# Level products of a gated recurrence in 32 by 32 blocks, and three fill products moved

## The reference

```python
b = cumsum(log_f, axis=1)
decay = exp(where(causal, b[:, :, None] - b[:, None, :], -inf))
scores = einsum('btshd,bshd->bhts', q[:, :, None] * decay, k)
o = einsum('bhts,bshv->bthv', scores, v) + einsum('bthd,bhdv->bthv', q * exp(b), state)
new_state = exp(b_end)[..., None] * state + einsum('bshd,bshv->bhdv', k * exp(b_end[:, None] - b), v)
```

## Time and profile before

| | |
|---|---|
| runs of the kernel before | 2424.71, 2426.08, 2427.40 us (median 2426.08) |
| profiled execution | 2427.41 us; its span, first to last instruction, 2425.6 us |
| TensorE busy | 2325.3 us, 96% |
| VectorE, ScalarE, GpSimd busy | 1211.8, 703.2, 644.4 us |
| mean granted TensorE clock | 0.984 of 2.4 GHz |

### The profile page before, as it was taken

One profiled execution on the slowest core, in us unless ns is written; L12 is line 12 of the kernel. 1 busy time (PEld: TensorE's weight loads), 2 busy tenths in 40 slices (PEclk: granted clock), 3 DMA queues, 4 the chain that ended last, 5 costly groups with the idle time before them and its releaser, 6 DMA issues. The chain is left out here.

```text
span 2425.6 us, 37166 instructions
## 1 busy us (share of the span) xinstructions
PE 2325.3 (96%) x14722; PEld 2194.6 (90%) x14722; DVE 1211.8 (50%) x2110; ACT 703.2 (29%) x1428; POOL 644.4 (27%) x725
## 2 busy tenths in 40 slices
PE   6999999999999999889999898979999999999997
PEld 6989999999999999778879898979899899898896
DVE  4125699999970776255543545154233233232335
ACT  5224412221221223344544323242122122121221
POOL 3453522122312876200001212142121212121213
PEclk9999999999999999999999999989999999999999
DMA  5351223232325443522116433231111111111104
GB/s 164 108 133 58 66 81 96 82 102 82 99 85 166 143 121 86 159 83 87 57 39 202 155 113 99 75 122 54 51 38 48 42 44 44 43 51 36 52 18 156
DMA packets 208951, 214.64 MB, mean 88 GB/s; under 512 B 32624, under 2 KB 190064, under 8 KB 208816
## 3 DMA queue, kind: packets, MB, share of 16 engines
q1 hardware_dynamic: 208816, 212.80, 28.1%
HBM read 153.34 MB, written 59.43 MB: 88 GB/s over the span
## 5 line engine op out<-in xcount | busy, mean ns | idle before, releaser
L249 POOL TENSOR_TENSOR w_lo<-w_raw,w_hi 128x2048 fp32r<-128x2048 f32 (+2 forms) x41 | 174.3, 4252 | 634.5 <-ACT w_hi L242 634.5
L2452 POOL TENSOR_TENSOR w_lo<-w_raw,w_hi 128x2048 fp32r<-128x2048 f32 x31 | 142.9, 4608 | 589.5 <-ACT w_hi L2476 589.5
L262 PE MATMUL ps<-f_hi,w_hi 128*128 128x384 f32 (+1 forms) x768 | 251.4, 327 | 2.4 <-POOL ff_u_lo L2448 2.4
L262 PE MATMUL ps<-f_hi,w_lo 128*128 128x384 f32 (+1 forms) x768 | 251.4, 327 | 0.0
L262 PE MATMUL ps<-f_lo,w_hi 128*128 128x384 f32 (+1 forms) x768 | 251.2, 327 | 0.0
L262 PE MATMUL ps<-h_hi,w_lo 128*128 128x384 f32 (+1 forms) x768 | 250.6, 326 | 0.0
L262 PE MATMUL ps<-h_lo,w_hi 128*128 128x384 f32 (+1 forms) x768 | 250.5, 326 | 0.0
L262 PE MATMUL ps<-h_hi,w_hi 128*128 128x384 f32 (+1 forms) x768 | 250.4, 326 | 0.0
L623 ACT ACTIVATE b_stage<-ps 128x256 f32<-128x256 f32 (+4 forms) x203 | 84.8, 418 | 526.6 <-PE ps L262 526.6
L2529 DVE TENSOR_TENSOR big<-big,ps 128x512 f32<-128x512 f32 x144 | 99.0, 688 | 271.9 <-PE ps L262 271.9
L262 PE MATMUL ps<-w_hi,h_hi 128*128 128x256 f32 (+1 forms) x792 | 226.2, 286 | 3.5 <-PEq L488 3.5
(11 more groups left out here) (226 smaller groups left out, 5475.1 us busy)
## 6 DMA issues: line engine op xcount, KB each, us to landing
w_raw<-in_w_in SPq DMA_DIRECT2D x34, 1024.0 KB, 5.5
w_raw<-in_w_up SPq DMA_DIRECT2D x16, 1024.0 KB, 5.3
w_raw<-in_w_down SPq DMA_DIRECT2D x16, 1024.0 KB, 5.1
gm_gate<-d_gate SPq DMA_DIRECT2D x48, 192.0 KB, 2.5
d_gate<-gatef_stage SPq DMA_DIRECT2D x28, 192.0 KB, 3.4
gm_y_raw<-d_y SPq DMA_DIRECT2D x8, 576.0 KB, 5.0
n_x<-in_x_prompt SPq DMA_DIRECT2D x8, 512.0 KB, 7.6
w_raw<-in_w_mem_kv SPq DMA_DIRECT2D x4, 1024.0 KB, 5.9
```

The costliest lines, as they stand in the source:

```text
L249: engine.tensor_tensor(g.w_lo[:, s, 0:size], g.w_raw[:, s, 0:size], g.w_hi[:, s, 0:size].bitcast(F32), ALU.subtract).then_inc(g.w_split, 1)
L262: last = pe.matmul(out, left(a, kk), right(b, kk), start=(kk == 0 and n == 0), stop=(kk == k - 1 and n == 2))
L2452: G.tensor_tensor(g.w_lo[:, slot, :], g.w_raw[:, slot, :], g.w_hi[:, slot, :].bitcast(F32), ALU.subtract).then_inc(g.w_split, 1)
```

## The change

Levels 1 to 16 are made as 32 by 32 products: for each head and each block of 32 tokens, keys of the block by queries of the block, written to that block's 32 output partitions and to columns j x 32 of the bank, so that one bank holds all six heads. One predicated copy a level, with masks of 32 columns, puts them into a compact tile `sdiag` (cleared once by GpSimd), and after level 16 VectorE copies the 4 (tile 8: 2) diagonal blocks from it into `smat` and signals `d_done`, for which the read-out now waits. Levels 32 and 64 are made as blocks of first-half keys by second-half queries and kept by plain copies, one for each block. A level takes one bank, and VectorE waits for its own copy of the level before. The masks are loaded by four DMAs. In the attention the 3 fill matmuls stand behind `mem_turn` and `q_turn`.

```diff
--- before.py
+++ after.py
@@ -1065,6 +1065,10 @@
     return levels(i) + ["q", "k"]
 
 
+DIAG = 32
+NEAR = [h for h in LEVELS if 2 * h <= DIAG]
+
+
 PER_TILE = len(LEVELS) + 2
 
 
@@ -1107,7 +1111,8 @@
         ybT = sb("ybT", [P, B_HEADS, P])
         ms, expo = sb("ms", [P, B_HEADS]), sb("expo", [P, B_HEADS])
         state = [sb("stateP", [P, B_HEADS, HD]), sb("stateS", [P, B_HEADS, HD])]
-        masks = sb("masks", [P, len(LEVELS) - 1, P], I32)
+        sdiag = sb("sdiag", [P, 2, B_HEADS, DIAG])
+        masks = sb("masks", [P, len(NEAR), DIAG], I32)
 
         sem = lambda name: g.sem("hr_" + name)
         masks_in, state_in, s_cleared = sem("masks_in"), sem("state_in"), sem("s_cleared")
@@ -1116,7 +1121,7 @@
         k_ready, q_ready = [sem("k_ready0"), sem("k_ready1")], [sem("q_ready0"), sem("q_ready1")]
         t_ready = [sem("t_ready0"), sem("t_ready1")]
         lv_done, lv_free, qk_done, qk_free = sem("lv_done"), sem("lv_free"), sem("qk_done"), sem("qk_free")
-        sq_done, rs_done, o_normed = sem("sq"), sem("rs"), sem("o_normed")
+        sq_done, rs_done, o_normed, d_done = sem("sq"), sem("rs"), sem("o_normed"), sem("d_done")
 
         LV_BANK, N_LV, QK_BANK, N_QK = 4, 4, 2, 2
 
@@ -1129,7 +1134,7 @@
             if tick in STEP_AT:
                 i, pos = STEP_AT[tick]
                 if pos < len(levels(i)):
-                    lv += 1 if pos == len(levels(i)) - 1 else 2
+                    lv += 1
                     lv_of[i, pos] = lv
                 else:
                     qk += 2
@@ -1185,7 +1190,9 @@
                 sp.dma_start(heads(wide(bg, i)), features(g.d_bg, i)).then_inc(v_in[i % 3], 16)
 
             load_first(0)
-            sp.dma_start(masks[:], io["c_masks"][:, 0:len(LEVELS) - 1, :]).then_inc(masks_in, 16)
+            for k0 in range(0, P, DIAG):
+                sp.dma_start(masks[k0:k0 + DIAG], io["c_masks"][k0:k0 + DIAG, 0:len(NEAR), k0:k0 + DIAG]
+                             ).then_inc(masks_in, 16)
             load_first(1)
             load_second(0)
             load_second(1)
@@ -1242,13 +1249,14 @@
                 k, q = heads(wide(key, i)), heads(wide(query, i))
                 pe.wait_ge(k_ready[i % 2], ready(i, pos))
                 pe.wait_ge(q_ready[i % 2], ready(i, pos))
-                if 2 * s == t:
-                    level_unit(range(B_HEADS), lambda bank, j, h: pe.matmul(
-                        bank[0:s, j * s:(j + 1) * s], k[:, h, 0:s], q[:, h, s:t], start=True, stop=True))
-                    return
-                for hs in halves:
-                    level_unit(hs, lambda bank, j, h: pe.matmul(
-                        bank[0:t, j * P:j * P + t], k[:, h, :], q[:, h, :], start=True, stop=True))
+                n, step, ahead = (DIAG, DIAG, 0) if s in NEAR else (s, 2 * s, s)
+
+                def make(bank, j, h):
+                    for k0 in range(0, t, step):
+                        last = pe.matmul(bank[k0:k0 + n, j * n:(j + 1) * n], k[:, h, k0:k0 + n],
+                                         q[:, h, k0 + ahead:k0 + ahead + n], start=True, stop=True)
+                    return last
+                level_unit(range(B_HEADS), make)
 
             def recur_read(i):
                 t, st = rows(i), state[i // TILE_P]
@@ -1261,6 +1269,7 @@
                 elif i:
                     pe.wait_ge(lv_free, lv_state[i - 1])
                 pe.wait_ge(lv_free, lv_of[i, n_lv - 1])
+                pe.wait_ge(d_done, i + 1)
                 q = heads(wide(query, i))
 
                 def make(out, h):
@@ -1355,6 +1364,7 @@
         @stage.gpsimd
         def _(pool):
             G.memset(expo[:], -0.5)
+            G.memset(sdiag[:], 0.0)
             G.memset(smat[:], 0.0).then_inc(s_cleared, 1)
 
             def q_start(i):
@@ -1446,23 +1456,25 @@
                 t, s = rows(i), levels(i)[pos]
                 if i == 0 and pos == 0:
                     dve.wait_ge(s_cleared, 1)
-                    dve.wait_ge(masks_in, 16)
+                    dve.wait_ge(masks_in, 16 * (P // DIAG))
                 if i >= 2 and pos == 0:
                     dve.wait_ge(qk_done, qk_of[i - 2, "q"])
-                if 2 * s == t:
-                    n = lv[0]
-                    bank = level_bank()[0:s, 0:B_HEADS * s].rearrange("p (h t) -> p h t", h=B_HEADS)
-                    dve.wait_ge(lv_free, n)
-                    V.tensor_copy(smat[0:s, i % 2, :, s:t], bank).then_inc(lv_free, 1)
-                    return
-                m = bcast_mid(masks[0:t, LEVELS.index(s), 0:t], H3)
-                for j in range(2):
-                    n = lv[0]
-                    bank = level_bank().rearrange("p (h t) -> p h t", h=H3)
-                    if n >= 2:
-                        dve.wait_ge(lv_free, n - 1)
-                    V.copy_predicated(smat[0:t, i % 2, j * H3:(j + 1) * H3, 0:t], m,
-                                      bank[0:t, :, 0:t]).then_inc(lv_free, 1)
+                if pos:
+                    dve.wait_ge(lv_free, lv_of[i, pos - 1])
+                n, held = (DIAG, sdiag[0:t, i % 2]) if s in NEAR else (s, None)
+                bank = level_bank()[0:t, 0:B_HEADS * n].rearrange("p (h t) -> p h t", h=B_HEADS)
+                if s in NEAR:
+                    m = bcast_mid(masks[0:t, NEAR.index(s), :], B_HEADS)
+                    V.copy_predicated(held, m, bank).then_inc(lv_free, 1)
+                else:
+                    for k0 in range(0, t, 2 * s):
+                        last = V.tensor_copy(smat[k0:k0 + s, i % 2, :, k0 + s:k0 + 2 * s], bank[k0:k0 + s])
+                    last.then_inc(lv_free, 1)
+                if s == NEAR[-1]:
+                    dve.wait_ge(lv_free, lv_of[i, pos])
+                    for k0 in range(0, t, DIAG):
+                        last = V.tensor_copy(smat[k0:k0 + DIAG, i % 2, :, k0:k0 + DIAG], held[k0:k0 + DIAG])
+                    last.then_inc(d_done, 1)
 
             def keep_state(i):
                 st, eb = state[i // TILE_P], total(i, rows(i))
@@ -1783,11 +1795,11 @@
                     prob_out(n - 3)
                 if slot == 4 and i < N_TILE:
                     mem_out(i)
-                fl.fill(pe, PER_SLOT[1])
                 if slot == 3 and i < N_TILE:
                     mem_turn(i)
                 if slot == 5 and i + 1 < N_TILE:
                     q_turn(i + 1)
+                fl.fill(pe, PER_SLOT[1])
                 if 2 <= n < N_HEAD + 2:
                     prob_turn(n - 2)
             fl.fill(pe, len(fl.units) * fl.n_mm)
```

## The result

The changed kernel takes **2397.86 us** (median; 2394.84 to 2399.11), the kernel before 2425.96 beside it: ratio 0.9878 [0.9864, 0.9892], faster by 1.2%. The profiled execution took 2397.91 us.

A forecast was written before the change was run, and what follows sets the result against it. TensorE's own instructions were taken to bound the recurrence. Levels +15.6, attention -6 and first stall -1.3 gave +8.3 us: 2435.7 profiled, 2434.4 median, slower by 0.34%, range 2392 to 2470.

The forecast's parts named there:

- the price of a narrow pass: Recurrence, level products: 32-column passes start 0.032 us apart on TensorE, so the levels cost +15.6 us.
- the forecast's own formula: Recurrence levels on TensorE: 2232 p added for passes, 53 x 0.26 for entering and leaving narrow form, 69.6 us removed.
- the rival: Recurrence levels: four partition groups run side by side, p at 0.016, levels -20, all -27, 2399 us; chance 0.33.
- p: Interval between narrow passes on TensorE in the recurrence: taken as 0.032 us, bounds 0.008 and 0.064, break-even at 0.025.
- the first stall: Recurrence, TensorE's one 1.6 us wait for VectorE, at tile 1's reciprocal: 1.3 us of it cancelled.
- the 25 us that VectorE was to save: Recurrence: cheaper predicated copies less diagonal copies save VectorE 3.2 us a tile, some 25 us over eight tiles.
- the cover stays: Recurrence: VectorE's work lies hidden behind TensorE, its saving too except at the first stall; no new waits priced.
- The attention: Fills moved behind the memory and query transposes fit into TensorE's waits for ScalarE's copies: -6 us, bounds 0 and -8.5.
- the query places: Attention, slot 5: three fills fit into the gap behind the query transposes, 8 places x 0.49 = 3.9 us gained.
- the memory places: Attention, slot 3: three fills fit into the waits behind the memory transposes, 9 x 0.45 = 4.0 us gained.
- The stall given back at the normalised probabilities: Attention: fills no longer cover the memory transposes' wait for VectorE's normalised probabilities, so 0.9 us of gain is lost.
- the main case: Whole kernel: narrow passes at 0.032 us make it slower, 2434 us, own range 2429 to 2444; chance 0.45.

The follow-up runs named there:

- one-group run: Changed kernel with loops reordered, all heads of one token block before the next, so neighbouring passes go to the same 32 output partitions: 2422.76 us, ratio 0.9983.
- run with half copies: Kernel before the change, with VectorE's predicated copies cut to the first half of each head's queries: 2425.23 us, ratio 0.9994.

## Why the prediction was wrong

**The step that failed is the price of a narrow pass**: "I take 0.032, the nearest row". That row holds twelve passes to one group of output partitions. It was read rightly, as the one-group run shows (31 to 32 ns inside a group), but it says nothing of passes that go round four groups. The reasoning, "weight loads that go in order with the products would keep that rate whatever group they are for", made a rule of a case with one group. Measured: 0.0092 at four groups and 0.016 at two, near the lower bound that I had put (0.008, fully side by side); in the even part of a block it is that bound, 32 ns for four passes. By the forecast's own formula:

- 40 levels of 48 passes at 0.0092 are 17.7 us, 13 levels of 24 at 0.016 are 5.0; with 53 x 0.26 - 69.6 this gives -33.1.
- The levels in the two traces, from the last fill before to the second fill behind and without waits, differ by -23.65 us for the 40 levels 1 to 16, -4.98 for the eight levels 32 and -1.70 for tile 8's five, together -30.3. The 2.8 us between are the cost of going in and out, 0.31 a level instead of 0.26.
- TensorE's waits in the recurrence grew from 2.8 to 6.9 us: -26.2, beside -25.7 read from the marks.

That the time fell on the 2399 of the rival is in part luck. The rival had p at 0.016, which gave -20 us for the levels, -6 for the attention and -1.3 at the first stall; the traces have -30.3, -4.2 and +4.1 us of waits.

**Rule against rule.** The Trainium skill ("TensorE: Matmul & The Clock Gate", Part 3) has a weight load overlap running products only where the row group differs. Here every pass uses all 128 rows, and 48 loads and 48 products fit into 0.63 us, the loads starting as close to each other as the products: the trace goes against that rule for passes of different column groups. The Trainium skill's "TensorEngine Tiling (Array Packing)", Key Properties (tiles load weights and multiply in parallel), agrees with it. I gave the rival that rests on it 0.33 because no row spoke of a change of group; that was an open question between two bounds, and the even row of one group was no evidence on either side of it.

**VectorE.** The copies' prices were right where they read PSUM (367 ns and, for the 32-row blocks, 347). But the 25 us that VectorE was to save did not come: it is busy for 2.3 us less in this stage. Three things were wrong. Two predicated copies in a row took 50.9/48 = 1.06 us of its time, not 2 x 0.584 = 1.17, which takes 5 us off the saving. The diagonal copies cost 518 ns each and not 339, since that row reads PSUM and the new copies go from SBUF to SBUF beside GpSimd. And the key updates, which the forecast left out, took 655 ns on the mean and now take 734 (those by the forget gate 968 and 1560). In the one-group run, with the same instructions on both engines, the key update takes 664 ns and the diagonal copy 398: the faster pace of TensorE seems to bring more of VectorE's work beside GpSimd's, which is argued and was not tested by itself. That a saving would have been hidden is right, as the run with half copies shows. Wrong again was that the cover stays: with levels 0.58 us shorter, TensorE's ticks no longer hide VectorE, and the waits for it rose from 1.6 to 4.7 us. The forecast of -1.3 at the first stall came out as 0 there (still 1.6).

**The attention** gave -4.0 to -4.2 us instead of -6: the query places as worked out, the memory places nothing that can be measured. The stall given back at the normalised probabilities was named and priced at 0.9 (measured 1.0); what remained of the memory places' 4.0 did not come.

**Right**: the count of passes, the predicated copies, the clock (1.00 from 810 us), GpSimd's added clear and the four mask loads, neither of which shows in any wait; 45 predicated copies instead of 106; and the test named beforehand, a block shorter than 1.4 us, which at 0.63 tells the main case wrong in sign.

## What to carry to other kernels

Products with few output columns on all 128 rows are cheap only if consecutive passes go to different 32-column groups: order the loops so that the group changes fastest (one loop order was worth 25 us here), and expect to pay 0.3 us for each block that goes from the full form into the narrow one and back. When TensorE's step gets shorter, price the neighbours again: VectorE, whose relief by 20 us was worth nothing before, cost nearly the whole gain once it had 15 us more to do afterwards; copies between SBUF tiles on VectorE beside a busy GpSimd are the first to try on ScalarE (2.3 to 6.5 us here). A price taken from the nearest row holds for what that row does; where the new work differs from it in just the property in dispute, it says nothing for either side, and the chances should be near even.

## What the runs showed of the hardware

- Full-row fp32 passes of 32 columns: in the even part of a block 0.032 us apart within one column group, 0.016 with two groups in turn, 0.008 with four; with 64 columns 0.058 in one and 0.029 in two. Whole blocks with their ends: 0.033 (12 passes), 0.014 to 0.016 and 0.009, with 64 columns 0.062 and 0.030. In the four-group block single starts stand 7, 7, 6 and 12 ns apart for the first 33 passes, but for one of 33 ns behind the first four, and then mostly in pairs 17 ns apart; the starts of the weight loads stand as close.
- Where the order changes group only three times in 48 passes, 0.1 us is saved around each change: seven starts take 0.122 us instead of 0.224.
- A wait of 3.39 us of TensorE inside the recurrence was followed by the 1.2 GHz level (a mean of 0.66 over the 10 us around it), where waits of up to 1.6 us in the changed kernel left it at 1.00: a wait can cost more than its length.
- A VectorE copy of 32 x 192 fp32 from SBUF to SBUF takes 0.25 us undisturbed and up to 1.88 when it meets a GpSimd operation; the same copy on ScalarE took 0.35 to 0.37 in both of its runs.
